# A two-block sequence kernel: the state-space parameters of both layers worked out together, from the start of the program

## The chip, the cores and the metric

The kernel runs on one core of a Trainium2 chip. Its time is the device time of one execution in microseconds (us); the median over several runs counts. Engines are called as in the profile: PE is TensorE, DVE is VectorE, ACT is ScalarE, POOL is GpSimd, SP is SyncE, which here only issues transfers.

## What is computed

A stack of two blocks over a sequence of 512 positions with 1024 features, float32. The first block has two layers. Each normalises x, multiplies it by a wide input matrix, and feeds the pieces to three branches: sliding-window attention, a gated short convolution and a state-space model. Their gated sum goes through another matrix and is added to x; a feed-forward part follows. The second block (long convolution and differential attention) is not touched here. What matters is the state-space branch, with 32 groups of 64 states per layer:

```python
for i in range(DEPTH):                       # DEPTH = 2
    h = rmsnorm(x, norm_mix[i])
    proj = h @ w_in[i]
    ...
    ys = gelu(s5_ssm(u, ssm_a_re[i], ssm_a_im[i], ssm_b_re[i], ssm_b_im[i], ssm_c_re[i], ssm_c_im[i], ssm_d[i], ssm_log_dt[i]))
def s5_ssm(u, a_re, a_im, b_re, b_im, c_re, c_im, d, log_dt):
    lam = lax.complex(a_re, a_im)
    dt = jnp.exp(log_dt)[:, None]
    lam_bar = jnp.exp(lam * dt)
    b_bar = ((lam_bar - 1.0) / lam)[..., None] * b_c
    bu = jnp.einsum("blgh,gph->blgp", uf, b_bar)
    _, states = lax.associative_scan(combine, (a_elems, bu), axis=1)
    y = jnp.einsum("blgp,ghp->blgh", states, c_c).real
```

Step width (`dt`), angle and size of `lam_bar`, its powers 1 to 3 and the input factor `(lam_bar - 1) / lam` with its powers depend on the weights only, not on x. There are 32 x 64 of each per layer, held as 128 partitions x 16 columns.

## The kernel before, in words

**Matrix products.** Weights come in units of 512 KB (128 x 1024 float32) into four slots. SP issues the load (L199), ACT writes a rounded copy `w_hi` (L206), POOL writes the rest `w_lo = raw - w_hi` (L211), and PE multiplies three times per 128 x 128 piece: high with high, high with low, low with high (L232 to L234). A slot is loaded again when its rest is made, and rounded again when PE has used it.

**mixer1**, once per layer, walks over groups of output columns in the hand-written order of `order1()`: groups 0 and 1 are the two halves of u (the input of the state-space branch), then cc, cx, cb of the convolution, and so on. Every engine has its own program, a walk over the same groups, and instructions of an engine run in the order in which they are written. Where the state-space pieces stand is set by tables: `MATRICES_AT`, `INPUTS_AT`, `STATES_AT` and others, by group number. Two groups share the accumulator banks 0 to 3, so group 2 can start only when DVE has taken group 0 out.

**Start of the layer on each engine.** The input of the product is x times the norm's gain, not yet divided by the root of the mean square: ACT writes `h_hi` (L288) and squares (L291), DVE `h_lo` (L297) and the sum of squares (L303). In layer 1 only the last four of eight tiles are done here (behind L987). PE runs group 0, adds up the squares over partitions (L262), DVE makes the mean (L268), POOL the power -1/2 (L272), PE spreads it over the partitions (L278) amid group 1, ACT copies the row out (L326, semaphore `row_kept`). From there on everything uses the true norm: DVE makes the normed tiles (L337), ACT rounds them (L332), DVE writes their rest (L344) and takes u out of the banks times the row (L1044, `take_u`). `take_u(0)` is what PE's group 2 waits for.

**State-space parameters**, between L268 and L337 on DVE, in tiles `col` of 128 x 16: half the gate's bias and three constants (L995 to L998); with ACT's exponential of `log_dt` (L822) the angle and the real part (L1001, L1002), ten operations that bring the angle into range (L1004 to L1012), behind which wait ACT's two sines (L827, L828); the multiplier and two powers (L1015 to L1025, helper `times`: six operations for a complex product); the fourth power's size and angle (L1030 to L1035). After `take_u` and the first turns (L1062): fourteen operations for the input factor (L1069 to L1082), two copies, and four complex products in a row (L1020 to L1025 again). Then `c_matrices(0)` (L1104 to L1109) builds what PE needs in `matrices(0)` (L633, then L640 after a wait for `c_powers`), and the product of group 3 (L1275) follows on DVE. All of it stands in both layers. DVE, ACT and PE wait for all eight small loads of L580 (`small_in`), the parameters `par` first among them.

A DVE operation signals and DVE waits for it before the next one (`Count.done`).

## Time and profile before

| | us |
|---|---|
| median of 3 runs | 2878.67 |
| lowest and highest run | 2877.82, 2880.61 |
| profiled execution, its own time | 2883.49 |
| span of its instructions | 2881.4 |
| PE busy in the span | 2658.4 (92%) |
| DVE busy | 1515.8 (53%) |
| POOL busy | 1120.7 (39%) |
| ACT busy | 921.6 (32%) |

The profiled execution is one run of its own; its time lies 2.1 us above its span and 4.8 us above the median. Busy shares are means over stages with different limits; the mean granted PE clock was 0.949 of 2.4 GHz.

### The profile page before, as it was taken

The numbers are of one execution on the slowest core, as the hardware profiler recorded it, in microseconds if no ns is written. First come the engines' busy times: TensorE is split into PE (matmuls) and PEld (weight loads), VectorE is DVE, ScalarE is ACT, GpSimd is POOL, SyncE is SP. The second block draws the span as 40 slices with busy tenths as digits, with TensorE's granted clock in tenths as the row PEclk, the third lists the DMA queues.
The fourth block names the chain that finished last, engine by engine and source line by source line (L and its number), as shares of the span: only waits on it lengthen the run. The fifth ranks groups of instructions, "written<-read, shape, count | busy, mean of one in ns | idle before, by whom it ended". The sixth has DMA issues, their size and how long they took to land. (4 is left out here: it accounts for less than half of the span.)

```text
span 2881.4 us, 32544 instructions
## 1 busy us (share of the span) xinstructions
PE 2658.4 (92%) x12732; PEld 2104.3 (73%) x12732; DVE 1515.8 (53%) x1891; ACT 921.6 (32%) x1310; POOL 1120.7 (39%) x507
## 2 busy tenths in 40 slices
PE   6899999999998899999999998699999888699995
PEld 4677777788887677777788887587776667488884
DVE  7985434743435996435663333598544542532334
ACT  4232433322223332343322222343334432222221
POOL 3233333344433324333344443278721113244332
PEclk9999999999999899999999999799989988799998
DMA  4222222343334212222334332232211102123321
GB/s 159 59 59 85 68 79 88 100 149 117 116 120 131 59 59 74 82 68 81 110 121 140 127 124 74 95 93 74 83 53 47 44 22 88 52 95 102 95 87 37
DMA packets 226635, 253.40 MB, mean 88 GB/s; under 512 B 9040, under 2 KB 202960, under 8 KB 226256
## 3 DMA queue, kind: packets, MB, share of 16 engines
q1 hardware_dynamic: 226192, 251.18, 27.8%
q8 instruction: 83, 1.36, 0.2%
q10 hardware_dynamic: 320, 0.52, 0.1%
q14 instruction: 40, 0.33, 0.0%
HBM read 246.96 MB, written 4.19 MB: 87 GB/s over the span
## 5 line engine op out<-in xcount | busy, mean ns | idle before, releaser
L211 POOL TENSOR_TENSOR sb_w_lo<-sb_raw,sb_w_hi 128x1024 fp32r<-128x1024 f32 x404 | 982.7, 2444 | 1493.9 <-ACT sb_w_hi L206 1492.0
L232 PE MATMUL ps<-sb_a_hi,sb_w_hi 128*128 128x512 f32 x1472 | 608.8, 414 | 48.0 <-DVE sb_u L1044 26.6
L206 ACT ACTIVATE sb_w_hi<-sb_raw 128x1024 fp32r<-128x1024 f32 x404 | 422.9, 1056 | 619.7 <-PE ps L234 541.0
L233 PE MATMUL ps<-sb_a_lo,sb_w_hi 128*128 128x512 f32 x1472 | 591.7, 402 | 0.0
L234 PE MATMUL ps<-sb_a_hi,sb_w_lo 128*128 128x512 f32 x1472 | 591.0, 401 | 0.0
L232 PE MATMUL ps<-sb_b_hi,sb_w_hi 128*128 128x512 f32 x960 | 382.2, 398 | 10.1 <-PEq L183 4.3
L232 PEld LDWEIGHTS ps<-sb_a_hi,sb_w_hi 128*128 128x128 f32 x1472 | 283.2, 192 | 147.8 <-issue 32.0
L233 PE MATMUL ps<-sb_b_lo,sb_w_hi 128*128 128x512 f32 x960 | 381.1, 397 | 0.0
L234 PE MATMUL ps<-sb_b_hi,sb_w_lo 128*128 128x512 f32 x960 | 380.8, 397 | 0.0
L234 PEld LDWEIGHTS ps<-sb_a_hi,sb_w_lo 128*128 128x128 f32 x1472 | 282.3, 192 | 69.7
L233 PEld LDWEIGHTS ps<-sb_a_lo,sb_w_hi 128*128 128x128 f32 x1472 | 282.9, 192 | 65.8 <-issue 2.4
L232 PE MATMUL ps<-sb_f_hid_hi,sb_w_hi 128*128 128x512 f32 x608 | 243.2, 400 | 4.8 <-issue 2.4
L233 PE MATMUL ps<-sb_f_hid_lo,sb_w_hi 128*128 128x512 f32 x608 | 242.6, 399 | 0.0
L234 PE MATMUL ps<-sb_f_hid_hi,sb_w_lo 128*128 128x512 f32 x608 | 241.8, 398 | 0.0
L232 PEld LDWEIGHTS ps<-sb_b_hi,sb_w_hi 128*128 128x128 f32 x960 | 181.0, 189 | 57.3 <-issue 8.0
L234 PEld LDWEIGHTS ps<-sb_b_hi,sb_w_lo 128*128 128x128 f32 x960 | 181.1, 189 | 44.3
L233 PEld LDWEIGHTS ps<-sb_b_lo,sb_w_hi 128*128 128x128 f32 x960 | 181.1, 189 | 43.5
L1823 DVE TENSOR_TENSOR sb_a_hi<-sb_a_hi,ps 128x2048 f32<-128x2048 f32 x32 | 73.2, 2288 | 157.1 <-PE ps L234 157.1
L2341 DVE SCALAR_TENSOR_TENSOR ps<-sb_m_u,sb_m_pr,ps 128x512 f32<-128x512 f32 x192 | 145.1, 756 | 6.8
L232 PEld LDWEIGHTS ps<-sb_f_hid_hi,sb_w_hi 128*128 128x128 f32 x608 | 115.6, 190 | 33.8 <-issue 2.8
L234 PEld LDWEIGHTS ps<-sb_f_hid_hi,sb_w_lo 128*128 128x128 f32 x608 | 115.6, 190 | 28.3
L233 PEld LDWEIGHTS ps<-sb_f_hid_lo,sb_w_hi 128*128 128x128 f32 x608 | 115.6, 190 | 27.6
(339 smaller groups left out, 2960.5 us busy)
## 6 DMA issues: line engine op xcount, KB each, us to landing
sb_raw<-in_w_in_dram SPq DMA_DIRECT2D x148, 512.0 KB, 3.8
sb_raw<-in_w_ffn_in_dram SPq DMA_DIRECT2D x88, 512.0 KB, 5.1
sb_raw<-in_w_ff_dram SPq DMA_DIRECT2D x64, 512.0 KB, 3.9
sb_ada<-in_w_ada_dram SPq DMA_DIRECT2D x48, 512.0 KB, 4.3
sb_raw<-in_w_ffn_out_dram SPq DMA_DIRECT2D x44, 512.0 KB, 3.8
sb_raw<-in_w_mix_o_dram SPq DMA_DIRECT2D x16, 512.0 KB, 3.4
sb_raw<-in_w_conv_o_dram SPq DMA_DIRECT2D x8, 512.0 KB, 3.7
sb_raw<-in_w_attn_o_dram SPq DMA_DIRECT2D x8, 512.0 KB, 3.5
```

The lines of the kernel that those rows point to most:

```text
L206: act.activation(w_hi[:, s, :], raw[:, s, :], ACT.Copy).then_inc(hi_done[s], 1)
L211: pool.tensor_tensor(w_lo[:, s, :], raw[:, s, :], w_hi[:, s, :].bitcast(F32), ALU.subtract)\
L232: pe.matmul(out, wh, hi, start=first and i == 0, stop=False)
L233: pe.matmul(out, wh, lo, start=False, stop=False)
L234: ins = pe.matmul(out, wl, hi, start=False, stop=last and i == len(rhs) - 1)
L1823: df.done(tt(out, out, ps[:, 4:8, :], ALU.add))
L2341: ins = stt(acc, src, w, acc, ALU.mult, ALU.add)
```

## The change

- New tiles for both layers, made once: `par1` (128 x 2 x 96), `cols`, `powers`, `g_powers`, `biases`. Intermediates of 32 columns (two layers x 16) lie in two tiles of `b_lo`, which is free then.
- One transfer of both layers' parameters, `par1`, is issued first of all, ahead of the gains and x (semaphore `par_in`). The load of `par` in each layer is gone.
- Layer 0, DVE: `turn_angles()` (20 operations) before the first `h_lo`; `multipliers()` (16) between the mean and the wait for the row; `input_factors()` (25) where the 40 operations were. The powers of the input factor come from three factors at a time (six operations of 96 columns) and one more product, not from four products in a row.
- Layer 0, ACT: the two exponentials before the gains and x, the two sines after the first rounded weight unit, ahead of tile 4 of x.
- Layer 1: none of it. Neither DVE nor ACT waits for the small loads there; PE waits for seven.

```diff
@@ mixer1, sync
                         if l == 0:
+                            sp.dma_start(par1[:, :, :], d["par1"].rearrange("l p n -> p l n")).then_inc(par_in, 16)
                             sp.dma_start(gains[:, :], d["gains"][:, :]).then_inc(gains_in, 16)
...
-                        for t, src in ((par[:, :], d["par1"][l, :, :]), (rot[:, :], d["const"][:, CONST["rot1"][0]:CONST["rot1"][1]]),
+                        for t, src in ((rot[:, :], d["const"][:, CONST["rot1"][0]:CONST["rot1"][1]]),
@@ mixer1, tensor
-                                    pe.wait_ge(small_in, 8 * 16)
-                                    pe.wait_ge(par_dve, 3)
+                                    pe.wait_ge(small_in, 7 * 16)
+                                    if l == 0:
+                                        pe.wait_ge(par_dve, 3)
@@ mixer1, scalar
                                 act.wait_ge(x_in[kt], 16)
                                 if kt == 4:
                                     prefetch(1)
+                                    act.wait_ge(par_dve, 2)
+                                    pa.done(act.activation(SN, TAU, ACT.Sin, scale=TURN))
+                                    pa.done(act.activation(CS, PHC, ACT.Sin, scale=-TURN))
...
                         if l == 0:
+                            pa = Count(act, par_act)
+                            act.wait_ge(par_in, 16)
+                            pa.done(act.activation(DT, both_layers("log_dt", 16), ACT.Exp))
+                            act.wait_ge(par_dve, 1)
+                            pa.done(act.activation(MAG, RD, ACT.Exp))
                             act.wait_ge(gains_in, 16)
                         act_rest(act, rest, gain, h_hi, ga, ready)
-                        prefetch(SLOTS)
-                        pa = Count(act, par_act)
-                        act.wait_ge(small_in, 8 * 16)
-                        pa.done(act.activation(DT, pcol("log_dt", 0, 16), ACT.Exp))
-                        act.wait_ge(par_dve, 1)
-                        pa.done(act.activation(MAG, RD, ACT.Exp))
                         prefetch(SLOTS + 1)
-                        act.wait_ge(par_dve, 2)
-                        pa.done(act.activation(SN, TAU, ACT.Sin, scale=TURN))
-                        pa.done(act.activation(CS, PHC, ACT.Sin, scale=-TURN))
                         act_keep_row(act, trig[:, 0, 0:T])
@@ mixer1, vector
+                            turn_angles()
                             dve.wait_ge(gains_in, 16)
                         dve_rest(dve, step, rest, gain, h_hi, h_lo, ga)
                         dve_mean(dve, SUM_BANK, 0, cm)
-                        dve.wait_ge(small_in, 8 * 16)
...
+                        step.done(dve.memset(z[:, :, 0:2], 0.0))
+                        if l == 0:
+                            multipliers()
 
                         dve.wait_ge(row_kept, 1)
...
                         step.done(dve.memset(xo[:, :, :, 0:1], 0.0))
-                        step.done(ts(LR, LAM[0][0], -1.0, None, ALU.add))
...
-                        for i in range(1, STEP + 1):
-                            times(G[i], G[i - 1], LAM[0])
+                        if l == 0:
+                            input_factors()
```

The new functions, without the arithmetic that is as before:

```python
def multipliers():
    dve.wait_ge(par_act, 4)
    step.done(tt(LAM[0][0], MAG, CS, ALU.mult))
    step.done(tt(LAM[0][1], MAG, SN, ALU.mult))
    for i in range(1, STEP - 1):
        times(LAM[i], LAM[i - 1], LAM[0], (tmp[:, 0, 0, :, :], tmp[:, 1, 0, :, :]), pd if i == STEP - 2 else None)
    step.done(tt(MAG4, MAG, MAG, ALU.mult))
    step.done(tt(MAG4, MAG4, MAG4, ALU.mult))

def input_factors():
    ...
    shape = [P, STEP - 1, DEPTH, 16]
    times([g_powers[:, part, :, :, 1:STEP].rearrange("p l s n -> p n l s") for part in range(2)],
          [f.unsqueeze(1).to_broadcast(shape) for f in first],
          [powers[:, part, :, :, :] for part in range(2)], [tmp[:, part, :, :, :] for part in range(2)])
    times([g_powers[:, part, :, :, STEP] for part in range(2)],
          [g_powers[:, part, :, :, 1] for part in range(2)], LAM[STEP - 2],
          [tmp[:, part, 0, :, :] for part in range(2)])
```

**ACT at the start of layer 0.** Before, up to the first four weight units and the exponentials (`sb_a_hi<-sb_x` is `h_hi`, `sb_b_hi<-sb_x` the squares, `sb_w_hi` a rounded weight unit, `sb_col` the parameters):

```order
L288 ACT_TABLE_LOAD
L288 ACTIVATE sb_a_hi<-sb_x,sb_gains 128x512 x4
L206 ACTIVATE sb_w_hi<-sb_raw 128x1024
L288 ACTIVATE sb_a_hi<-sb_x,sb_gains 128x512 x4
L291 ACTIVATE sb_b_hi<-sb_x 128x512 x8
L206 ACTIVATE sb_w_hi<-sb_raw 128x1024 x3
L822 ACTIVATE sb_col<-sb_par 128x16
```

Now, with the parameters in `sb_b_lo` and lines of the changed file:

```order
L834 ACT_TABLE_LOAD
L834 ACTIVATE sb_b_lo<-sb_par 128x32
L836 ACTIVATE sb_b_lo<-sb_b_lo 128x32
L294 ACTIVATE sb_a_hi<-sb_x,sb_gains 128x512 x4
L212 ACTIVATE sb_w_hi<-sb_raw 128x1024
L826 ACT_TABLE_LOAD
L826 ACTIVATE sb_b_lo<-sb_b_lo 128x32
L827 ACTIVATE sb_b_lo<-sb_b_lo 128x32
L294 ACTIVATE sb_a_hi<-sb_x,sb_gains 128x512 x4
L297 ACTIVATE sb_b_hi<-sb_x 128x512 x8
L212 ACTIVATE sb_w_hi<-sb_raw 128x1024 x4
L342 ACTIVATE sb_trig<-ps 128x512
```

The exponentials moved ahead of x. A table load and two sines now stand ahead of tiles 4 to 7 of x, the squares and the second weight unit. The fifth weight unit no longer has parameters before it.

**DVE in layer 1, around the mean.** Before, the mean (L268) and the first of the 37 instructions that stood between it and L337:

```order
L303 TENSOR_TENSOR sb_b_hi<-sb_b_hi 128x512 x4
L268 TENSOR_SCALAR sb_rstd<-ps 128x4
L995 TENSOR_SCALAR sb_bias<-sb_par 128x24
L996 MEMSET sb_bias 128x1
L997 MEMSET sb_bias 128x1
L998 MEMSET sb_bias 128x1
L1001 TENSOR_TENSOR sb_col<-sb_par,sb_col 128x16
L1002 TENSOR_TENSOR sb_col<-sb_par,sb_col 128x16
L1004 TENSOR_SCALAR sb_col<-sb_col 128x16
```

Now, from the mean (L274) to the first c matrices (L1129):

```order
L274 TENSOR_SCALAR sb_rstd<-ps 128x4
L1076 MEMSET sb_m 128x2x2
L353 SCALAR_TENSOR_TENSOR sb_b_hi<-sb_x,sb_gains,ps 128x512 x4
L360 TENSOR_TENSOR sb_a_lo<-sb_b_hi,sb_a_hi 128x512 x4
L353 SCALAR_TENSOR_TENSOR sb_b_hi<-sb_x,sb_gains,ps 128x512 x4
L1087 TENSOR_TENSOR sb_u<-ps,sb_trig 128x1024
L360 TENSOR_TENSOR sb_a_lo<-sb_b_hi,sb_a_hi 128x512 x4
L1087 TENSOR_TENSOR sb_u<-ps,sb_trig 128x1024
L1105 TENSOR_TENSOR sb_b_hi<-sb_trow,sb_cols 128x512
L1110 MEMSET sb_b_lo 128x512
L1111 MEMSET sb_b_lo 128x8
L1129 TENSOR_TENSOR sb_b_hi<-sb_cT,sb_g_powers 128x640
```

One memset is left between the mean and the normed tiles (L353), and none of the forty factor operations stand before L1129. In layer 0 the sixteen operations of `multipliers()` follow L1076, and the 25 of `input_factors()` stand before L1129.

## Rows read from the trace of the kernel before

**Rows 1.** What PE waited for, whole run: line, releaser, us in total, times, longest.
```profile
PE ps L232 <- DVE sb_u L1044: 26.6, 2, 13.3
PE ps L640 <- DVE sb_qkv L1109: 11.5, 2, 6.1
```
**Rows 2.** Timeline of DVE, layer 1: start us, us, engine, line, out<-in.
```profile
918.27 0.16 DVE L268 TENSOR_SCALAR sb_rstd<-ps 128x4 f32<-128x4 f32 x1 [1.83 <-PE ps L262]
...
930.81 3.10 DVE L337 SCALAR_TENSOR_TENSOR sb_b_hi<-sb_x,sb_gains,ps 128x512 f32<-128x512 f32 x4
...
951.06 0.17 DVE L1069 TENSOR_SCALAR sb_col<-sb_col 128x16 f32<-128x16 f32 x1
...
974.71 0.82 DVE L1109 SCALAR_TENSOR_TENSOR sb_qkv<-sb_b_hi 128x640 f32<-128x640 f32 x1
```
**Rows 3.** Timeline of PE, then of ACT, layer 1.
```profile
920.91 1.05 PE L278 MATMUL ps<-sb_ident,sb_rstd 128*128 128x128 f32 x8
...
943.64 0.79 PE L232 MATMUL ps<-sb_a_hi,sb_w_hi 128*128 128x512 f32 x1 [13.28 <-DVE sb_u L1044]
...
968.63 1.52 PE L633 MATMUL ps<-sb_ident,sb_col 128*32 128x128 f32 x48
975.58 1.11 PE L640 MATMUL ps<-sb_qkv,sb_trig 128*32 128x128 f32 x16 [5.44 <-DVE sb_qkv L1109]
...
1016.01 3.48 PE L669 MATMUL ps<-sb_u,sb_b_lo 128*128 128x512 f32 x8 [3.33 <-DVE sb_b_lo L1165]
...
924.28 0.60 ACT L326 ACTIVATE sb_trig<-ps 128x512 f32<-128x512 f32 x1
```
**Rows 4.** Timeline of ACT, start of layer 0.
```profile
5.54 1.28 ACT L288 ACT_TABLE_LOAD   x1 [5.54 <-DMA sb_x<-in_xT_dram]
...
18.34 1.05 ACT L206 ACTIVATE sb_w_hi<-sb_raw 128x1024 fp32r<-128x1024 f32 x1
...
34.44 0.21 ACT L828 ACTIVATE sb_col<-sb_col 128x16 f32<-128x16 f32 x1
```
**Rows 5.** Timeline of SP, start; then transfers issued from 895 to 960 us: KB, us to landing.
```profile
2.20 0.40 SPq L567 DMA_DIRECT2D sb_gains<-in_gains_dram  x1
...
sb_par<-in_par_dram SPq DMA_DIRECT2D x1, 48.0 KB, 1.8
```
**Rows 6.** Timeline of PE, layer 0.
```profile
21.91 0.50 PE L232 MATMUL ps<-sb_a_hi,sb_w_hi 128*128 128x512 f32 x1 [0.48 <-POOL sb_w_lo L211]
...
78.45 1.52 PE L633 MATMUL ps<-sb_ident,sb_col 128*32 128x128 f32 x48
86.04 1.10 PE L640 MATMUL ps<-sb_qkv,sb_trig 128*32 128x128 f32 x16 [6.07 <-DVE sb_qkv L1109]
```
**Rows 7.** Timeline of POOL, then of DVE, layer 0: the same stretch.
```profile
31.33 2.38 POOL L211 TENSOR_TENSOR sb_w_lo<-sb_raw,sb_w_hi 128x1024 fp32r<-128x1024 f32 x1 [1.38 <-ACT sb_w_hi L206]
...
31.35 2.39 DVE L1010 TENSOR_SCALAR sb_col<-sb_col 128x16 f32<-128x16 f32 x1
```
**Rows 8.** Timeline of DVE, layer 0.
```profile
28.68 0.16 DVE L268 TENSOR_SCALAR sb_rstd<-ps 128x4 f32<-128x4 f32 x1 [4.83 <-PE ps L262]
...
41.21 3.10 DVE L337 SCALAR_TENSOR_TENSOR sb_b_hi<-sb_x,sb_gains,ps 128x512 f32<-128x512 f32 x4
...
61.47 0.17 DVE L1069 TENSOR_SCALAR sb_col<-sb_col 128x16 f32<-128x16 f32 x1
...
78.84 0.83 DVE L1104 TENSOR_TENSOR sb_b_hi<-sb_cT,sb_gk 128x640 f32<-128x640 f32 x1
```
**Rows 9.** Timeline of DVE, then of POOL, just before layer 1.
```profile
893.67 2.29 DVE L1622 TENSOR_TENSOR sb_x<-sb_x,ps 128x2048 f32<-128x2048 f32 x1 [12.77 <-PE ps L234]
...
894.80 2.41 POOL L211 TENSOR_TENSOR sb_w_lo<-sb_raw,sb_w_hi 128x1024 fp32r<-128x1024 f32 x1 [3.19 <-ACT sb_w_hi L206]
```
**Rows 10.** Stretches of 4 us, PE: us, busy (instructions), granted clock, DMA share, GB/s.
```profile
88.00:92.00 4.00, 4.00 (x11) 0.50 0.00 0
...
96.00:100.00 4.00, 4.00 (x19) 1.00 0.02 2
```

More of the change, by code:

```diff
@@ L633, in matrices @@
                                         pe.matmul(ps[32 * j:32 * j + 32, 6 + part, n * P:(n + 1) * P],
[L634 removed]
+                                                  LAM[STEP - 2 - n][part][:, l, s:s + 1].to_broadcast([P, 32]), ident[:, :],
                                                   start=True, stop=True)
@@ new lines, in times @@
+                        def times(out, a, b, t, last=None):
+                            t0, t1 = t
+                            step.done(tt(t0, a[0], b[0], ALU.mult))
+                            step.done(tt(t1, a[1], b[1], ALU.mult))
+                            step.done(tt(out[0], t0, t1, ALU.subtract))
+                            step.done(tt(t0, a[0], b[1], ALU.mult))
+                            step.done(tt(t1, a[1], b[0], ALU.mult))
+                            (last or step).done(tt(out[1], t0, t1, ALU.add))
@@ new lines, in multipliers @@
+                        def multipliers():
+                            dve.wait_ge(par_act, 4)
+                            step.done(tt(LAM[0][0], MAG, CS, ALU.mult))
+                            step.done(tt(LAM[0][1], MAG, SN, ALU.mult))
+                            for i in range(1, STEP - 1):
+                                times(LAM[i], LAM[i - 1], LAM[0], (tmp[:, 0, 0, :, :], tmp[:, 1, 0, :, :]),
+                                      pd if i == STEP - 2 else None)
+                            step.done(tt(MAG4, MAG, MAG, ALU.mult))
+                            step.done(tt(MAG4, MAG4, MAG4, ALU.mult))
@@ new lines, in input_factors @@
+                        def input_factors():
+                            a_re, a_im = both_layers("a_re", 16), both_layers("a_im", 16)
+                            first = [g_powers[:, part, :, :, 0] for part in range(2)]
+                            LR, TA, TB, DEN = TH, RD, DT, TAU
+                            step.done(ts(LR, LAM[0][0], -1.0, None, ALU.add))
+                            step.done(tt(DEN, a_re, a_re, ALU.mult))
+                            step.done(tt(TA, a_im, a_im, ALU.mult))
+                            step.done(tt(DEN, DEN, TA, ALU.add))
+                            step.done(dve.reciprocal(DEN, DEN))
+                            step.done(tt(TA, LR, a_re, ALU.mult))
+                            step.done(tt(TB, LAM[0][1], a_im, ALU.mult))
+                            step.done(tt(TA, TA, TB, ALU.add))
+                            step.done(tt(first[0], TA, DEN, ALU.mult))
+                            step.done(tt(TA, LAM[0][1], a_re, ALU.mult))
+                            step.done(tt(TB, LR, a_im, ALU.mult))
+                            step.done(tt(TA, TA, TB, ALU.subtract))
+                            step.done(tt(first[1], TA, DEN, ALU.mult))
+                            shape = [P, STEP - 1, DEPTH, 16]
[5 more added lines that the diff above has]
+                                  [tmp[:, part, 0, :, :] for part in range(2)])
@@ L1018, in times @@
-                        def times(out, a, b):
-                            step.done(tt(TC, a[0], b[0], ALU.mult))
-                            step.done(tt(TD, a[1], b[1], ALU.mult))
-                            step.done(tt(out[0], TC, TD, ALU.subtract))
-                            step.done(tt(TC, a[0], b[1], ALU.mult))
-                            step.done(tt(TD, a[1], b[0], ALU.mult))
-                            step.done(tt(out[1], TC, TD, ALU.add))
-                        for i in range(1, STEP - 1):
-                            times(LAM[i], LAM[i - 1], LAM[0])
```

95 lines of the change are left out of this document (40 added, 55 removed).

## The prediction

> **What bounds the kernel now.** The page's busy shares come first: PE works 92% of the span, so time can only be won where PE stands still, or lost where it is made to. Next comes the list of what PE waited for. The two waits of 13.3 us for `take_u` of L1044, one per layer, and the two of about 6 us for the c matrices of L1109 are the places that this change touches [rows 1]; in both DVE is what is late. The timelines then show the order. In layer 1 the mean is made at 918.27 and the normed tiles start at 930.81: 12.54 us that are nothing but parameters [rows 2]. Yet the spread of L278 is done at 920.91 + 1.05 = 921.96, and the row copy of 0.60 us waited on ACT behind the two sines, until 924.28 [rows 3]. PE's group 2 restarts at 943.64 after 13.28 us. Behind it, DVE spends from 951.06 on the input factor, up to the c matrices, which end at 974.71 + 0.82 = 975.53, while PE has been waiting for 5.44 us [rows 2, 3]. Layer 0 has the same picture [rows 6, 8].
>
> One more thing sets DVE's pace: while POOL makes the rest of a weight unit, a DVE operation of 0.17 us can take as long as POOL's, as 2.39 beside 2.38 us from the same moment on [rows 7]. A DVE operation that reads a bank of PS is not held: 2.29 us for 2048 columns, with a unit of POOL starting in its midst [rows 9]. The Trainium skill gives the reason ("SBUF — State Buffer", Who interferes with whom): a VectorE instruction with two SBUF inputs and a GpSimd instruction that reads SBUF exclude each other for the whole instruction. By that rule, the rows agree.
>
> **Layer 1.** All 77 parameter operations of DVE (37 ahead of L337, 40 ahead of L1104) go, and so do ACT's four and the wait for the small loads. What is late next is the row: the spread ends at 921.96, ACT copies for 0.60, and DVE can start L337 at about 922.6 in place of 930.81, 8.2 us earlier [rows 2, 3]. From L337 to `take_u(0)` the work is the same. One unit of POOL falls into it as before, because ACT rounds that unit between the normed tiles; L337 itself reads PS and isn't held. So PE restarts at 943.64 - 8.2 = 935.4, after 5.1 us of standing still, not 13.3.
>
> PE then gets to the end of group 3 at 968.63 - 8.2 = 960.4 [rows 3]. DVE, which has neither the first nor the second set, would finish `c_matrices(0)` at 975.53 - 8.2 less the factors. Their 40 operations with POOL's stalls took from 951.06 to the first c matrix. Layer 0 has the same stretch, 61.47 to 78.84: 17.4 us [rows 8]. That gives 950, or 954 if two more stalls of 2.4 fall in, before PE asks. So the wait of 5.44 goes whole. DVE now waits for PE at the product of group 3, which it used to start at 975.56: it starts at 960.4 or a little later, 15.1 earlier. From there to the next wait of PE, 1016.01, DVE is the one that is late (PE waits 3.33 us there [rows 3]), so this place moves with DVE's 15.1, not only with PE's 8.2 + 5.4 = 13.6. PE would be there in time: it arrived at 1012.68, now at 999.1, and the low clock behind the old wait, which I price below, goes too. **Layer 1: -15.1 us.** The sine table, loaded before at L827, is loaded ahead of the first sines of the walk instead, 1.28 us; in the list of waits no one waits for those sines, so nothing.
>
> **Layer 0, start.** SP issues one more transfer ahead of x; its neighbour, the gains, takes 0.40 us to issue [rows 5]. Everything that lands shifts by that, or a little more for twice the rows: I take 0.5. At the other end the 96 KB could also cost x twice what 48 KB took to land, 2 x 1.8 = 3.6 us [rows 5]; nearer is the issue, since the transfers overlap. The first table load (1.28) and the exponentials use the time in which ACT waited for x anyway, until 5.54 [rows 4]. The twenty DVE operations of `turn_angles` take 20 x 0.23 = 4.6 us from about 5 on; DVE has nothing to do before ACT's first `h_hi`, and PE asks for `h_lo` only when POOL has made the first weight unit's rest, so I cost them at nothing; without that cover they would add up to 4.6. But behind the first weight unit ACT has a table load and two sines, 1.28 + 2 x 0.21 + gaps, some 1.8 us, and it is a chain without a gap from there to the second weight unit of 18.34 [rows 4]. That unit released PE at 21.91, after 0.48 of waiting [rows 6]. So unit 1, the sums, the mean and the spread come 0.5 + 1.8 = 2.3 us later. I see no gap between a table load and the activation behind it. The Trainium skill ("ScalarE: Activation LUTs", What ACT_TABLE_LOAD costs) adds a drain of about 1.38 us to every switch of set. By that the delay would be 3.7 and the total below 1.4 us less; the trace shows no such gap, so 2.3 stands.
>
> **Layer 0, first set.** A 16-column operation takes 0.17 us, one of 640 columns 0.83 [rows 8]: (0.83 - 0.17) / 624 is 1.06 ns a column, so 32 columns take 0.19, 96 take 0.26, and with the 0.04 us to the next 0.23 and 0.30. The mean comes at 28.68 + 2.3 = 31.0. The sixteen operations of `multipliers` are 16 x 0.23 = 3.7 us. POOL's fifth unit starts right behind the power of L272, about 32.3, its sixth behind the row copy, about 36.4. DVE is in two-input operations both times, so two stalls of 2.4 us: end at 31.3 + 3.7 + 4.8 = 39.8, against 41.21 [rows 8]. The row itself is there at 35.3. With neither stall it would be 35.3, and **-5.9**; I take **-1.4**, since POOL's units start where the operations are. PE's group 2 restarts 1.4 earlier, having stopped 2.3 later.
>
> **Layer 0, second set.** It starts at 61.47 - 1.4 = 60.1. Nineteen operations of 32 columns and six of 96: 19 x 0.23 + 6 x 0.30 = 6.2 us. POOL has the fraction of the turns, a weight unit right behind it and another some 1 us later, all still in this stretch: 2.4 + 2.4 + 2.1 of stalls. End at 73.0 in place of 78.84. `c_matrices(0)` took 7.1 us with one stall; now two fall in, 9.5: 82.5 in place of 86.0. PE gets there at 78.45 + 1.52 - 1.4 = 78.6 and still waits [rows 6]. DVE and PE leave together, so **layer 0: -3.5 us**. Bounds: -9 if two stalls fewer are met, +1 if x lands 3.6 late.
>
> The sum is -15.1 - 3.5 = **-18.6 us**, all of it carried to the end, since behind both places PE, DVE and the loads keep their order and PE has no slack to swallow it. The profiled execution would go from 2883.49 to 2864.9; its own time is 4.8 above the median, and the median 2878.67 goes to **2860**.
>
> **The rivals.**
> 1. *Fewer collisions with POOL, and a warmer clock.* At the low level (1.2 GHz, 0.50 granted) PE gets through 11 matmuls in 4 us, at 2.4 GHz through 19 [rows 10]; it fell after 13 and after 5 to 6 us of standing still and stayed low for some 5 us of work, so a fall costs about 2.3. If the restart of layer 1 after 5.1 us finds the clock still high, that is 2.3 more; two stalls fewer in layer 0 are 4.8 more. Together -25.7: 2853. For it: the idle time shrinks below what preceded the other falls. Against: a wait of 5.44 us was enough [rows 3]. Chance 0.17.
> 2. *Layer 1 gives only PE's first part, layer 0 nothing.* If DVE meets stalls anew behind the product of group 3, because POOL's units now fall on other operations, the 15.1 shrinks to 8.2, and the start of layer 0 eats the rest: 2870. For it: POOL holds DVE in most of its units here. Against: POOL is fed by ACT, which is fed by the same DVE and PE steps, so the pattern should move along. Chance 0.20.
> 3. *Next to nothing.* x lands 3.6 us late, four stalls fall into layer 0, and the row in layer 1 is late because ACT rounds the fifth unit first and that load lands late, behind the small loads, up to the 924.28 at which the row was copied before: 2874 to 2883. Chance 0.05.
> 4. *Slower: the clock.* The granted clock falls behind the small matmuls of the state-space part where a short wait precedes them. Such a block stands four times per layer. If the changed timing gave each of these eight a fall of its own at 2.3 us plus a wait as long as the 1.3 to 3.3 seen, it would cost up to 8 x 4 = 32 us, and from five such blocks on the 18.6 are gone: 2892 at worst, 2886 with six and a half. For it: PE and DVE run closer together. Against: DVE is earlier everywhere. Chance 0.02.
> 5. *The change doesn't do what it says*, a table or wait left in place. The instruction order shows one memset between mean and normed tiles in layer 1. Chance 0.01, 2878.
>
> **How the numbers follow.** The forecast has 0.55 for 2853 to 2867; rivals 1 to 5 have the rest. A measurement can tell about 0.2%, 5.8 us. Faster by more: the forecast, rivals 1 and 2, nearly all: 0.93. Within: 0.05. Slower: 0.02. The range takes in rival 1 and most of rival 2, from 2851 to 2869; outside lie rivals 3 to 5 and the tails.
>
> **What would show it.** In the changed profile: layer 1's normed tiles 4 us behind the mean, PE's wait for `take_u` near 5 us, no wait for c matrices, DVE idle before the product of group 3. Layer 0: PE's second unit 2 to 2.5 us later with a wait of some 2.5 us for POOL, PE's wait for `take_u` near 9.5, for the c matrices near 4. It would be wrong if layer 1's wait for `take_u` stayed above 8 us, if the place of L669 came less than 13 us earlier within layer 1, or if PE's second unit came over 4 us late.

## The result, and the profile after

The changed kernel takes 2860.14 us (median of 4 runs, 2857.8 to 2864.27), the kernel before beside it 2879.64 us (median of 4, 2877.82 to 2882.61). The ratio is 0.9933, 95% interval 0.9916 to 0.9950: 19.5 us faster, where 18.6 were forecast. The profiled execution is the slowest of its four: 2864.27 us, span 2862.2, mean granted clock 0.952 (before 0.949). PE is busy for 2657.4 us, before for 2658.4, so nearly all of the gain is time in which PE no longer stands still. One execution of one kernel below took 4125.85 us at a mean granted clock of 0.589, where every other one of the changed kernels took 2852 to 2881 us; it is in no median or comparison.

What PE waited for, whole run: line, releaser, us in total, times, longest. L1087 is `take_u`, before L1044. The c matrices are L1134, before L1109:

```profile
PE ps L238 <- DVE sb_u L1087: 11.9, 2, 8.8
PE ps L680 <- DVE sb_b_lo L1190: 7.5, 2, 4.9
```

The first line was 26.6 us [rows 1]. The wait for the c matrices, 11.5 us before, is left in layer 0 alone (3.7, below). The second line is what is late next: 4.9 us in layer 1, where it was 3.3 [rows 3].

DVE in layer 1, from the mean to the product of group 3:

```profile
914.70 0.16 DVE L274 TENSOR_SCALAR sb_rstd<-ps 128x4 f32<-128x4 f32 x1 [1.84 <-PE ps L268]
914.93 0.06 DVE L1076 MEMSET sb_m<- 128x4 f32 x1
919.12 3.10 DVE L353 SCALAR_TENSOR_TENSOR sb_b_hi<-sb_x,sb_gains,ps 128x512 f32<-128x512 f32 x4 [4.13 <-ACT sb_trig L342]
922.25 2.56 DVE L360 TENSOR_TENSOR sb_a_lo<-sb_b_hi,sb_a_hi 128x512 fp32r<-128x512 f32 x4
...
937.31 0.83 DVE L1129 TENSOR_TENSOR sb_b_hi<-sb_cT,sb_g_powers 128x640 f32<-128x640 f32 x1
...
945.80 2.91 DVE L1134 SCALAR_TENSOR_TENSOR sb_qkv<-sb_b_hi 128x640 f32<-128x640 f32 x1
952.63 1.23 DVE L1300 TENSOR_TENSOR sb_m<-ps,sb_m 128x1024 f32<-128x1024 f32 x1 [3.92 <-PE ps L240]
```

Where DVE worked for 12.54 us [rows 2] it now waits 4.13 us for the row. It has made the c matrices by 948.7, and then waits for PE. PE over the same stretch:

```profile
902.36 0.47 PE L238 MATMUL ps<-sb_a_hi,sb_w_hi 128*128 128x512 f32 x1 [1.17 <-PEq L189]
...
929.88 0.50 PE L238 MATMUL ps<-sb_a_hi,sb_w_hi 128*128 128x512 f32 x1 [3.10 <-DVE sb_u L1087]
...
952.47 1.52 PE L644 MATMUL ps<-sb_ident,sb_powers 128*32 128x128 f32 x48
953.80 0.66 PE L651 MATMUL ps<-sb_qkv,sb_trig 128*32 128x128 f32 x16
...
993.93 2.71 PE L680 MATMUL ps<-sb_u,sb_b_lo 128*128 128x512 f32 x3 [4.87 <-DVE sb_b_lo L1190]
```

The first row is PE's first matmul of layer 1; it stood at 905.94 before, so layer 0 gave 3.6 us in this pair of profiles. Counted from that row, the restart of group 2 stands at +27.5 (before +37.7) and L680 at +91.6 (before, L669, at +110.1): 10.2 and 18.5 us. A later place in the mixer, called the mark below, is PE's first matmul on `c_pair` behind a pause of 5.04 us; there 17.1 of them are left (+413.3 against +430.5). PE's restart is different in kind, too: its first matmul took 0.50 us and not 0.79 [rows 3], though not in every profile of this code (below).

PE in layer 0:

```profile
25.56 0.51 PE L238 MATMUL ps<-sb_a_hi,sb_w_hi 128*128 128x512 f32 x1 [1.64 <-POOL sb_w_lo L217]
...
53.26 0.79 PE L238 MATMUL ps<-sb_a_hi,sb_w_hi 128*128 128x512 f32 x1 [8.84 <-DVE sb_u L1087]
...
83.33 1.10 PE L651 MATMUL ps<-sb_qkv,sb_trig 128*32 128x128 f32 x16 [3.72 <-DVE sb_qkv L1134]
```

The second weight unit comes 3.65 us later than before, the restart 0.8 earlier, the c matrices 2.7 earlier [rows 6]. ACT at the start shows why the second unit is late:

```profile
2.21 1.28 ACT L834 ACT_TABLE_LOAD   x1 [2.21 <-PEq L189]
...
8.54 1.36 ACT L294 ACTIVATE sb_a_hi<-sb_x,sb_gains 128x512 fp32r<-128x512 f32 x2 [0.50 <-DMA sb_x<-in_xT_dram]
12.37 1.06 ACT L212 ACTIVATE sb_w_hi<-sb_raw 128x1024 fp32r<-128x1024 f32 x1 [2.47 <-DMA sb_x<-in_xT_dram]
13.44 1.28 ACT L826 ACT_TABLE_LOAD   x1
14.74 0.23 ACT L826 ACTIVATE sb_b_lo<-sb_b_lo 128x32 f32<-128x32 f32 x1
15.00 0.23 ACT L827 ACTIVATE sb_b_lo<-sb_b_lo 128x32 f32<-128x32 f32 x1
...
21.89 1.05 ACT L212 ACTIVATE sb_w_hi<-sb_raw 128x1024 fp32r<-128x1024 f32 x1
```

From the first rounded unit to the second it is 9.52 us; before it was 7.59 (10.75 to 18.34): 1.93 for the sines. The other 1.62 us is the first unit itself, 12.37 against 10.75, with ACT waiting 2.47 us just before it.

DVE's first set in layer 0, beside POOL:

```profile
32.32 0.16 DVE L274 TENSOR_SCALAR sb_rstd<-ps 128x4 f32<-128x4 f32 x1 [6.27 <-PE ps L268]
...
33.78 2.25 DVE L1025 TENSOR_TENSOR sb_b_lo<-sb_powers 128x32 f32<-128x32 f32 x1
...
37.88 2.28 DVE L1037 TENSOR_TENSOR sb_cols<-sb_b_lo 128x32 f32<-128x32 f32 x1
40.42 3.10 DVE L353 SCALAR_TENSOR_TENSOR sb_b_hi<-sb_x,sb_gains,ps 128x512 f32<-128x512 f32 x4
```
```profile
33.56 2.42 POOL L217 TENSOR_TENSOR sb_w_lo<-sb_raw,sb_w_hi 128x1024 fp32r<-128x1024 f32 x1
37.67 2.44 POOL L217 TENSOR_TENSOR sb_w_lo<-sb_raw,sb_w_hi 128x1024 fp32r<-128x1024 f32 x1 [1.69 <-ACT sb_w_hi L212]
```

Two operations of 0.19 us last until POOL's unit is done, the two stalls of the forecast. Profiled execution against profiled execution: 3.58 us from layer 0, 17.14 from layer 1, and behind that 1.5 us given back (the span's rest from the mark on is 1546.5 us, before 1545.0), together 19.2 of the 19.22 us measured. That rest is the same code in every kernel below, and took 1540.8 to 1546.5 us: 6 us of scatter. The experiments are therefore read by places counted from the start of the span or of layer 1, and by the whole time only where it was measured several times.

The start of layer 1 scatters too. The changed kernel and the four kernels of the next two sections have the same layer 0, and start layer 1 at 898.87 to 902.36 us; the changed kernel's own profile is the latest of the five. So layer 0's 3.6 us could be read as anything up to 7.1. Nearer to the edits, L680 of layer 0 stands at 122.47 to 123.91 in these five and at 126.52 before (L669): 2.6 to 4.1 us. What layer 0 gave is some 3 us, against one profile of the kernel before.

### The profile page after: what moved, and what is told of

The parts are those of the page before. It is cut to its first block and busy times, and to the rows that moved or that the text cites. A ratio compares the mean times of both kernels' runs of the same rounds, so it can differ in the third digit from the quotient of the medians.

```text
span 2862.2 us, 32440 instructions
## 1 busy us (share of the span) xinstructions
PE 2657.4 (93%) x12732; PEld 2104.1 (74%) x12732; DVE 1490.0 (52%) x1800; ACT 920.7 (32%) x1306; POOL 1122.7 (39%) x507
## 3 DMA queue, kind: packets, MB, share of 16 engines
HBM read 246.96 MB, written 4.19 MB: 88 GB/s over the span
```

## The experiments

Twelve runs of ten kernels, all made from the changed one. Each ratio is to runs of the kernel before on the same chip. The changed kernel's reference values: layer 1 starts at 902.36, restart +27.5, L680 +91.6, mark +413.3.

### What each set costs in layer 1

Small operations into an unused tile (the result stays as it is) take the place of the parameter work in layer 1: 36 where the first set stood, 40 where the second stood, or both.

```diff
                         if l == 0:
                             multipliers()
+                        else:
+                            for _ in range(36):
+                                step.done(tt(junk[:, :], pcol("a_re", 0, 16), pcol("a_im", 0, 16), ALU.mult))
...
                         if l == 0:
                             input_factors()
+                        else:
+                            for _ in range(40):
+                                step.done(tt(junk[:, :], pcol("a_re", 0, 16), pcol("a_im", 0, 16), ALU.mult))
```

> The changed kernel, but in layer 1 DVE makes 36 idle 16-column products of two SBUF tiles between the mean and the wait for the row, in the place of the first parameter set (they compute nothing that is used). Theory (DVE's two sets in layer 1 are what the gain came from): 36 x 0.21 us and two collisions with POOL, 12.2 us from mean to normed tiles in place of 4.4; counted from layer 1's first matmul, PE's group 2 restarts at 37.5 in place of 27.5 and the state-space wait for b_lo ends near 101.5 in place of 91.6; the time is 9 to 10 us above the changed kernel's. Rival (the waits for the small loads and ACT's exponentials and sines in layer 1 held it): these stay away, so less than 3 us are lost.

> The changed kernel with 40 such idle products in layer 1 where the input factors stood. Theory: DVE ends the c matrices 8.4 us plus two or three collisions later, 13 to 15 us, which is past the end of group 3; PE waits 8 to 10 us there and the place of the state-space wait comes 9 to 11 us later; the time is 9 to 11 us above the changed kernel's. Rival (PE's own work covers the second set once the first is gone): less than 3 us.

> Both sets of idle products in layer 1. Theory: both count, since DVE is late through the whole stretch: 17 to 19 us above the changed kernel, so 2877 to 2879, within 0.2% of the kernel before. Rival (the two hide each other, only the longer counts): as with one of them, 10 us above.

Measured, from layer 1's start to the mark, above the changed kernel: first set **13.1 us** (restart +37.35, after 12.94 us of waiting), second set **6.5 us** (restart unchanged, wait for the c matrices 7.45), both **18.2 us**, which is 431.5 us to the mark where the kernel before took 430.5. The whole: 2869.94 and 2864.17 in one profiled run each, and for both 2876.38 (median of 10, 2872.88 to 2880.97), ratio 0.9982, interval 0.9972 to 0.9991, to the kernel before. So with the idle work back in layer 1 nearly all of the gain is gone, without a single load, table or wait of the old kernel. What is left is layer 0's share.

PE in the first of them, then in the second:

```profile
936.22 0.79 PE L239 MATMUL ps<-sb_a_hi,sb_w_hi 128*128 128x512 f32 x1 [12.94 <-DVE sb_u L1091]
...
1002.90 4.40 PE L681 MATMUL ps<-sb_u,sb_b_lo 128*128 128x512 f32 x8 [4.87 <-DVE sb_b_lo L1194]
```
```profile
927.54 0.50 PE L239 MATMUL ps<-sb_a_hi,sb_w_hi 128*128 128x512 f32 x1 [3.10 <-DVE sb_u L1088]
959.10 1.10 PE L652 MATMUL ps<-sb_qkv,sb_trig 128*32 128x128 f32 x16 [7.45 <-DVE sb_qkv L1138]
...
999.59 3.35 PE L681 MATMUL ps<-sb_u,sb_b_lo 128*128 128x512 f32 x8 [3.33 <-DVE sb_b_lo L1194]
```

The first set was worth more than the 9.8 us by which it moved the restart (+37.35 against +27.5). It cost 12.5 at L680, counted from the start (+104.0), because PE then ran its next matmuls at the low clock (0.50 granted from 936 to 940 us). The second set cost 8.0 at L680 and 6.5 at the mark, less than the 9 to 11 expected and more than its rival's 3, since 3.9 us of DVE's waiting for PE took up a part of it, and PE's wait at L680 shrank from 4.87 to 3.33.

### Is it the operations, or what POOL does to them?

The 36 of the first place, with the second operand out of a bank of PS:

```diff
-                                step.done(tt(junk[:, :], pcol("a_re", 0, 16), pcol("a_im", 0, 16), ALU.mult))
+                                step.done(tt(junk[:, :], pcol("a_re", 0, 16), ps[:, 5, 0:16], ALU.mult))
```

> As the first run of this call, but each of the 36 idle products reads its second input from a bank of PS. Theory (POOL's weight units hold DVE operations with two SBUF inputs, not those with one): no operation of this set takes over 0.3 us, the set takes 8 to 9 us with no step of 2.3, the normed tiles start 4 to 5 us later than in the changed kernel and not 8. Rival (POOL holds DVE whatever it reads, or the long operations are a fetch of instructions): two operations of 2.3 us again, 8 us.

DVE's groups by line and shape from 905 to 960 us, busy and mean ns: the 36 with two SBUF inputs, then the 36 with one.

```profile
L1082 DVE TENSOR_TENSOR sb_junk<-sb_par 128x16 f32<-128x16 f32 x36 | 10.6, 296 | 1.2
```
```profile
L1082 DVE TENSOR_TENSOR sb_junk<-sb_par,ps 128x16 f32<-128x16 f32 x36 | 6.1, 171 | 1.2
```

As many operations of the same width take 10.6 us in one form and 6.1 in the other. From first to last it was 11.84 us against 7.34, and the normed tiles started at +24.5 and +20.0 (changed kernel +16.8). At the mark the second form costs 6.9 us and not 13.1. The whole time doesn't show it: 2869.21 us in one run, against 2869.94 of the first form, because in that profile layer 1 started 2.4 us later and the rest behind the mark took 3.0 us more. So at the normed tiles the first set costs 4.5 us for POOL's hold on DVE and 7.3 for the operations themselves, less the 4.1 us of waiting for the row. In both the first row of L361 took 4.64 us, not the 2.56 of the changed kernel: one POOL unit falls on it again, as before. That is the other 2.1 us of the restart, and the low clock behind it adds 2.6 in the first form and 1.7 in the second up to DVE's product of group 3 (25.4 and 24.5 us from the restart, 22.8 in the changed kernel).

### The start of layer 0

First, the early start undone and the rest kept: transfer (issued with the small loads again), exponentials, angles and sines behind the mean again, for both layers at a time. The diff shows what stands there now; the lines taken out of the start are left out.

```diff
@@ mixer1, scalar
                         act_rest(act, rest, gain, h_hi, ga, ready)
-                        prefetch(SLOTS + 1)
+                        prefetch(SLOTS)
+                        if l == 0:
+                            pa = Count(act, par_act)
+                            act.wait_ge(par_in, 16)
+                            pa.done(act.activation(DT, both_layers("log_dt", 16), ACT.Exp))
+                            act.wait_ge(par_dve, 1)
+                            pa.done(act.activation(MAG, RD, ACT.Exp))
+                        prefetch(SLOTS + 1)
+                        if l == 0:
+                            act.wait_ge(par_dve, 2)
+                            pa.done(act.activation(SN, TAU, ACT.Sin, scale=TURN))
+                            pa.done(act.activation(CS, PHC, ACT.Sin, scale=-TURN))
@@ mixer1, vector
-                            turn_angles()
                             dve.wait_ge(gains_in, 16)
...
                         if l == 0:
+                            turn_angles()
                             multipliers()
```

> Undoes the early start alone: both layers at a time in 32 columns, once, but all of angles and multipliers behind the mean of layer 0, exponentials and sines where they stood, the parameters loaded behind x. Theory: PE's second unit is released near 22 us again and the mean comes near 28.7, but 36 operations of 0.23, two collisions and the wait for the sines bring the normed tiles of layer 0 to 42.5 to 43, in place of 40.4: the early start is worth some 2 us, the time is 1.5 to 3 us above the changed kernel's. Rival A (the early start is a main part of the gain): 5 us or more above. Rival B (what it costs at the start eats it): equal or below.

The median is 2861.1 us (four runs, 2859.99 to 2862.38), ratio 0.9926, interval 0.9908 to 0.9944. The same kernel was run once more for its trace:

> The early start undone (all parameter work for both layers behind the mean of layer 0, the sets tiled over both layers as in the change), for a profile of it. Theory: PE's second unit at 22 to 23 us as in the kernel before, the mean 3 to 4 us earlier than in the changed kernel, and the width and angle work (some 5 us) between mean and row in its place, so layer 1 starts within 1.5 us of the changed kernel's 902.4 us and takes as long as there; the whole 2859 to 2863 us. Rival: the row waits for it all and layer 1 starts 3 us or more later.

That run took 2862.42 us. PE in layer 0:

```profile
54.21 0.79 PE L238 MATMUL ps<-sb_a_hi,sb_w_hi 128*128 128x512 f32 x1 [13.13 <-DVE sb_u L1090]
84.06 1.11 PE L651 MATMUL ps<-sb_qkv,sb_trig 128*32 128x128 f32 x16 [3.26 <-DVE sb_qkv L1137]
...
124.49 4.12 PE L680 MATMUL ps<-sb_u,sb_b_lo 128*128 128x512 f32 x8 [3.86 <-DVE sb_b_lo L1193]
```

The mean is 3.3 us earlier (28.99 against 32.32), the normed tiles 0.95 later (41.37), and layer 1 starts at 903.80, 1.4 later. Against all five profiles that have the early start, this one has the normed tiles 0.6 to 2.1 us later (they have them at 39.31 to 40.76) and L680 0.6 to 2.0 later. So the part of the change that its diff shows first, the early start, is worth some 1 us, 2 at most, by a single profile without it, and below what the whole time can tell. The gain is the work done once.

Then the sines into ACT's wait for the fifth tile of x, one kernel in two runs, the second timed six times:

```diff
+                                if kt == 4:
+                                    act.wait_ge(par_dve, 2)
+                                    pa.done(act.activation(SN, TAU, ACT.Sin, scale=TURN))
+                                    pa.done(act.activation(CS, PHC, ACT.Sin, scale=-TURN))
                                 act.wait_ge(x_in[kt], 16)
                                 if kt == 4:
                                     prefetch(1)
-                                    act.wait_ge(par_dve, 2)
-                                    pa.done(act.activation(SN, TAU, ACT.Sin, scale=TURN))
-                                    pa.done(act.activation(CS, PHC, ACT.Sin, scale=-TURN))
```

> The changed kernel with ACT's sine table and two sines put ahead of the wait for tile 4 of x, where ACT stood for 2.47 us. Theory: they cost nothing there; squares, second weight unit and PE's second unit come 1.8 us earlier (23.8 in place of 25.6), and so does everything of layer 0 behind them: 1.5 to 2 us below the changed kernel. Rival (the late second unit is due to x landing late alone): no change at PE's second unit.

> The changed kernel with the two sines ahead of the wait for the fifth x tile, once more and now timed in rounds. Theory: the sines in the gap give back the 2.2 to 2.5 us by which the changed kernel's second unit came later, 2856 to 2858 us against the 2860.1 of the changed kernel. Rival: the one look at 2855.8 us was scatter, 2859 to 2861 us.

ACT in the first of the two:

```profile
10.29 1.28 ACT L824 ACT_TABLE_LOAD   x1
11.58 0.23 ACT L824 ACTIVATE sb_b_lo<-sb_b_lo 128x32 f32<-128x32 f32 x1
11.85 0.23 ACT L825 ACTIVATE sb_b_lo<-sb_b_lo 128x32 f32<-128x32 f32 x1
12.11 1.06 ACT L212 ACTIVATE sb_w_hi<-sb_raw 128x1024 fp32r<-128x1024 f32 x1
...
19.69 1.05 ACT L212 ACTIVATE sb_w_hi<-sb_raw 128x1024 fp32r<-128x1024 f32 x1
```

The second unit is 7.58 us behind the first again, as before the change. The mean comes at 30.04 and 30.76 (31.02 to 32.66 in the five profiles with the sines in their old place), L680 of layer 0 at 121.29 and 122.23 (122.47 to 123.91): 1.6 us earlier by the means, as the first theory had it. Layer 1 starts at 897.81 and 896.75, 1.1 to 5.6 us earlier; that is more than L680 shows, but between the two places runs the same code, and it took 774.5 to 779.4 us over all profiles. The whole: 2855.82, and timed 2859.78 (median of 6, 2854.57 to 2862.33), which is in the rival's range and not in the 2856 to 2858 expected. The place gained some 1.6 us, the whole time can't show them.

Next the other suspect, the place of `par1` in SP's queue; here ACT issues it, so that nothing stands ahead of the gains and x:

```diff
@@ mixer1, sync
-                            sp.dma_start(par1[:, :, :], d["par1"].rearrange("l p n -> p l n")).then_inc(par_in, 16)
@@ mixer1, scalar
+                            act.dma_start(par1[:, :, :], d["par1"].rearrange("l p n -> p l n")).then_inc(par_in, 16)
                             act.wait_ge(par_in, 16)
```

> The changed kernel with the parameters' transfer issued by ACT, so that SP starts with the gains and x as in the kernel before. Theory (the issue ahead of x costs 0.5 us): tile 4 of x is there 0.5 us earlier and PE's second unit too. Rival (the 256 short rows themselves hold x up): tile 4 lands as late as in the changed kernel, or, if half of its 1.6 us was this, 1 us earlier.

2864.89 us in one run; first matmul of PE at 14.71 (15.90 in the changed kernel), second unit at 24.36 after 2.36 of waiting, but restart at 53.59 and layer 1's start at 902.04, as in the changed kernel. And the first matmul says little: over the ten profiles in which SP issues `par1` ahead of x it stood at 14.27 to 16.14, in the kernel before at 14.29. Whether the transfer delays x at all stays open; if so, it is within that scatter.

### A better place for the two sets in layer 0

DVE has nothing to do from 11.2 to 16.0 us in the changed kernel. First all 41 operations were put there, behind the fourth low part:

```diff
         def dve_rest(dve, steps, tiles, gain, h_hi, h_lo, sq, amid=None):
 
             for n, kt in enumerate(tiles):
+                if amid is not None and n == 4:
+                    amid()
...
+                        def amid():
+                            multipliers()
+                            input_factors()
...
-                        dve_rest(dve, step, rest, gain, h_hi, h_lo, ga)
+                        dve_rest(dve, step, rest, gain, h_hi, h_lo, ga, None if l else amid)
```

> Sines ahead of tile 4 as above, and on DVE multipliers and input factors in layer 0 between the fourth and the fifth low part of x, where DVE stood for 4.8 us. Theory (layer 0 is held by DVE after the mean as layer 1 was): mean near 30.5, normed tiles near 35 as soon as the row is there, PE's group 2 restarts 5.5 to 7.7 us earlier than in the changed kernel, and the wait of 3.7 us for the c matrices goes: 9 to 12 us below the changed kernel, near 2850. Rival (the start of layer 0 is held by loads, and what DVE does there delays PE's second unit): under 4 us below.

2858.78 us (median of 5, 2856.68 to 2861.96), ratio 0.9918: 1.4 us below the changed kernel by the medians, the rival's range. Not the 9 to 12 us, since the work moved from one wait of PE to another:

```profile
30.79 0.77 PE L238 MATMUL ps<-sb_a_hi,sb_w_hi 128*128 128x512 f32 x1 [8.44 <-DVE sb_a_lo L305]
```

With four stalls of 2.1 to 2.5 us the 41 take from 11.07 to 29.86, the next low parts come after them, and the mean at 39.98; PE's group 2 restarts at 55.18, later than the changed kernel's 53.26. So only the multipliers went there:

```diff
-                        dve_rest(dve, step, rest, gain, h_hi, h_lo, ga)
+                        dve_rest(dve, step, rest, gain, h_hi, h_lo, ga, None if l else multipliers)
...
                         step.done(dve.memset(z[:, :, 0:2], 0.0))
-                        if l == 0:
-                            multipliers()
```

> The sines stand ahead of the wait for the fifth x tile, and of the two sets only the multipliers (16 instructions, 5.7 us with one stall) go into layer 0's DVE idle time behind the fourth low part; the input factors stay where the change has them. My theory of the start (what DVE does ahead of the mean delays PE's second unit only by what does not fit in the idle time there, 2.7 us of it, and what it does between the mean and the row is paid in full): mean at 31 to 33 us, normed products 4.1 us behind it, at 35 to 37 us (38.1 in the run with the sines alone moved, 40.4 in the changed kernel), the wait at the first product of take_u 3 to 6 us, layer 1 starting 2 to 5 us earlier than with the sines alone, 2850 to 2854 us. Rival (the multipliers' place is as dear there as behind the mean, as the run with all 41 instructions there was): 2856 to 2860 us.

And beside it, with the factors split: their first 13 operations between mean and row, the complex products (12 operations) where the change has them.

```diff
                         step.done(dve.memset(z[:, :, 0:2], 0.0))
                         if l == 0:
-                            multipliers()
+                            input_factors()
...
                         if l == 0:
-                            input_factors()
+                            input_factor_powers()
```

> As the run beside it (sines in the gap, multipliers amid layer 0's low parts), and the first 13 instructions of the input factors (3.1 us, one stall with it 5.4) stand between the mean and the wait for the row, where DVE would else wait 4.1 us for ACT. Theory (work that fits a wait costs nothing): normed products at most 1.3 us later than in the run beside it, the piece left behind take_u shorter by 3 to 5 us, the c matrices of layer 0 earlier by 2 to 4 us, the whole 1 to 3 us below the run beside it. Rival (the row does not wait for the last of DVE's small work, PE's restart does): what is gained behind is lost ahead, within 1 us of the run beside it.

| | mean | normed tiles | c matrices asked: PE's wait | L680, layer 0 | layer 1 starts | median us (runs) |
|---|---|---|---|---|---|---|
| sines in the gap | 30.76 | 38.85 | 4.40 | 122.23 | 896.75 | 2859.78 (6) |
| and multipliers amid | 32.33 | 38.30 | 4.21 | 119.51 | 894.62 | 2860.64 (6) |
| and factors split | 32.18 | 38.14 | none | 114.59 | 891.07 | 2853.89 (4) |

The three ran on one chip. The last is 2853.89 us (2852.35 to 2855.38), ratio 0.9910, interval 0.9895 to 0.9924, to the kernel before (2880.92 there): the best version of this study, 27 us below before and some 6 below the changed kernel, by medians of separate sets of runs, whose intervals overlap (0.9916 to 0.9950 for the changed kernel). The places show it better: L680 of layer 0 comes 4.9 us earlier than in the run beside it, where 2 to 4 were expected. The multipliers alone gave 1.8 to 2.7 us there, and nothing in the whole time (2860.64, just above the rival's 2856 to 2860). DVE in the last:

```profile
32.18 0.16 DVE L274 TENSOR_SCALAR sb_rstd<-ps 128x4 f32<-128x4 f32 x1 [1.28 <-PE ps L268]
...
33.78 2.04 DVE L1053 TENSOR_TENSOR sb_b_lo<-sb_b_lo,sb_par 128x32 f32<-128x32 f32 x1
...
38.14 3.10 DVE L355 SCALAR_TENSOR_TENSOR sb_b_hi<-sb_x,sb_gains,ps 128x512 f32<-128x512 f32 x4 [0.68 <-ACT sb_trig L344]
```

The thirteen, with a stall, fit into the wait for the row, with 0.68 us to spare; without them that wait was 5.68. But the normed tiles did not come at 35 to 37 as expected. The row was late, for a reason none of the theories had. PE in the same run, first its rows, then stretches of 4 us (us, busy, instructions, granted clock):

```profile
31.05 1.02 PE L268 MATMUL ps<-sb_ones,sb_b_hi 128*128 128x1 f32 x8 [2.58 <-DVE sb_b_hi L311]
...
36.35 1.05 PE L284 MATMUL ps<-sb_ident,sb_rstd 128*128 128x128 f32 x8
...
48.91 0.50 PE L238 MATMUL ps<-sb_a_hi,sb_w_hi 128*128 128x512 f32 x1 [3.10 <-DVE sb_u L1094]
```
```profile
28.00:32.00 4.00, 1.42 (x11) 1.01 (x10) 2.80 (x4) 0.00 (x0) 0.18 (x1) 1.00 0.60 182
32.00:36.00 4.00, 4.00 (x12) 3.14 (x12) 3.52 (x9) 0.00 (x0) 3.36 (x2) 0.60 0.00 0
```

DVE's sums of squares are now 2.58 us late, and behind that pause PE runs at 0.60 granted, gets 12 matmuls done in 4 us and not 23 (in the run with the sines alone there is no pause, and both stretches are at 1.00), and comes to the spread 1.5 us later than there, counted from the mean (4.17 against 2.63 us; 4.19 in the run beside it, which has the same pause). PE's restart in turn waits 3.10 us and finds the clock high.

## Why the prediction was right, point by point

- **What bounds: right.** The gain is all in the waits that were named, and the idle operations put back in their places cost as much as the old ones: 431.5 us to the mark, before 430.5.
- **Layer 1, restart: 8.2 forecast, 10.2 measured.** The row sets the normed tiles, 4.4 us behind the mean, as worked out. The size was off since "one unit of POOL falls into it as before" failed. ACT rounds that unit when it has rounded the first four normed tiles. Before, it took these as DVE made them. Now DVE makes them while PE is still at group 1 and reads the tiles that ACT would write over, so ACT waits for PE first: PE works until 926.78 and the normed tiles start at 919.12, where before it had stopped at 930.36, ahead of their 930.81. ACT and then POOL, before:

```profile
931.65 1.35 ACT L332 ACTIVATE sb_a_hi<-sb_b_hi 128x512 fp32r<-128x512 f32 x2 [5.83 <-DVE sb_b_hi L337]
...
935.60 2.44 POOL L211 TENSOR_TENSOR sb_w_lo<-sb_raw,sb_w_hi 128x1024 fp32r<-128x1024 f32 x1 [7.29 <-ACT sb_w_hi L206]
```

  and now:

```profile
921.23 2.20 ACT L348 ACTIVATE sb_a_hi<-sb_b_hi 128x512 fp32r<-128x512 f32 x4 [1.26 <-PE ps L240]
...
924.45 2.63 POOL L217 TENSOR_TENSOR sb_w_lo<-sb_raw,sb_w_hi 128x1024 fp32r<-128x1024 f32 x1 [1.99 <-ACT sb_w_hi L212]
```

  POOL's unit starts 5.33 us behind the first normed tile and not 4.79, when DVE is at the last of its four low parts, and these take 2.56 us where they took 4.64. So the step that failed is "the pattern should move along", this time to the good.
- **Layer 1, the clock: rival 1's half, by luck.** The forecast left a low clock behind a wait of 5.1 us. The wait was 3.10 and the first matmul 0.50 us long, and PE reached the small matmuls of group 3 22.6 us after the restart (929.88 to 952.47), before 25.0 (943.64 to 968.63). That is the 2.3 of the rival, 2.4 by these rows. But eight profiles have this same layer 1 with this same wait, and in three of them the clock fell all the same (0.56, 0.65 and 0.71 granted in the 4 us around the restart; 24.0 to 25.3 us to the small matmuls, L680 at +93.0 to +94.3). With the clock as low as the forecast had it, the gain at L680 is 15.8 us and at the mark 15.4, close to its 15.1.
- **Layer 1, c matrices: right.** The wait went whole, although `c_matrices(0)` met three stalls (2.92, 2.91, 2.91), the one of before and two more, as in the forecast's later figure of 954; 3.9 us of slack are left.
- **Layer 1, L669: 15.1 forecast, 18.5 measured** (17.1 at the mark): the two terms above are 2.0 and 2.4, less 0.9 on the way from group 3 to L680 (41.3 us, before 40.5). "All of it carried to the end" did not hold: from L680 to the mark the eight profiles take 320.8 to 321.8 us, before 320.4.
- **Layer 0, start: 2.3 forecast, 3.65 measured.** The sines' 1.8 were 1.93. The 0.5 for the transfer was 1.62, of which the runs can't tell transfer from scatter. The first matmul of PE stands at 14.27 to 16.14 over the ten profiles with this order of transfers, so another profile could have given 2 us. No gap stood between table load and sine (0.02 us), so the drain of the Trainium skill ("ScalarE: Activation LUTs", What ACT_TABLE_LOAD costs) isn't seen here.
- **Layer 0, first set: -1.4 forecast, -0.8 measured**, two stalls as said; the start took the difference. Over the five profiles it is -0.5 to -1.9 (normed tiles at 40.76 to 39.31, before 41.21).
- **Layer 0, second set: -3.5 forecast, -2.7 at the c matrices, -3.6 by layer 1's start, -2.6 to -4.1 at L680 of the five.** Three stalls in the 25 operations as assumed, two in the c matrices as assumed (3.03 and 2.91). The forecast's own terms add up to 73.1 where it has 73.0. Its bounds don't follow from its terms either: two stalls of 2.4 fewer make -8.3 and not -9, and x landing 3.6 us late, 3.1 more than assumed, makes -0.4 and not +1.
- **POOL's hold on DVE.** "By that rule, the rows agree" was said too widely: the operation shown as held, L1010 [rows 7], is a TENSOR_SCALAR with one SBUF input, which the rule as cited there doesn't name. For two-input operations the idle products show it.
- **Rivals 2 to 5** didn't come. Rival 2's mechanism (stalls anew) exists, but fell on operations with slack behind them.

The mechanism was the one forecast: DVE's two sets in layer 1, and a smaller gain in layer 0. That the total came out 0.1 us from the forecast is luck. In the profiled execution layer 1 gave 2 us more than predicted and the rest of the program gave 1.5 back, and both the clock in layer 1 and the place where it starts vary by 2 us and more from one profile to the next.

## What to carry to other kernels

Work that depends on weights alone should be done once, at full width: 36 small operations cost what they take from first to last less the wait that they fill (7.7 us here). They cost 2.1 more because a unit of POOL then falls on DVE's next operations, and 2.6 more through PE's clock. Before moving such work, list the waits of its engine with their lengths, and put into each only what fits with a stall in it; 41 operations in a wait of 5 us moved PE's wait ahead, 13 in a wait of 5.7 us were free. Where a program's rest scatters by 6 us, read a gain of 2 by its place and not by the whole time, by a place close behind the edit, and in more than one profile.

## What the runs showed of the hardware

- POOL holds even the smallest two-input operations of DVE: 36 of 16 columns take 10.6 us, and 6.1 with one input in PS, as the rule cited in the prediction has it ("SBUF — State Buffer" of the Trainium skill). Yet a TENSOR_SCALAR with a single SBUF input was held as well (2.39 us beside a unit of 2.38) [rows 7], so two SBUF inputs are not the only case.
- The granted clock does not go by the length of the pause alone, nor by the program. Behind pauses of 8.4 to 13.3 us before group 2 the first matmul takes 0.79 us each time. Behind 3.10 us it takes 0.50 in most profiles and 0.79 in two, in the first run with the sines in the gap and in the one with ACT's transfer:

```profile
925.34 0.79 PE L238 MATMUL ps<-sb_a_hi,sb_w_hi 128*128 128x512 f32 x1 [3.10 <-DVE sb_u L1088]
```
```profile
929.55 0.79 PE L238 MATMUL ps<-sb_a_hi,sb_w_hi 128*128 128x512 f32 x1 [3.10 <-DVE sb_u L1087]
```

  Before the c matrices L651 takes 1.11 us behind a pause of 3.26 us, 0.68 and 0.67 behind one of 4.40 us (the two runs with the sines in the gap) and 0.66 without a pause. And behind a pause of 2.58 us in layer 0 the clock was still high and fell afterwards, to a mean of 0.60 over the next stretch.
- DVE operations of 32 columns take 0.19 us as expected, those of 96 take 0.33 and not 0.26; six of them, so 0.4 us.
